# Inputs laid out with channels in the partitions, a token half of a residual added early, and layers' operands made in two steps

## The reference

```python
# first block
h = rms_norm(x, g_mix_pre);  proj = h @ w_in            # 2048 -> 9728
aq, ak, av, hq, hf, hi, hg, gate_a, gate_b = split(proj)
y_attn = sliding_window_attention(rotary(aq), rotary(ak), av, sinks)
y_hgrn = rms_norm(hgrn2_recurrence(hq, hf, hi, lb)) * silu(hg)
merged = sigmoid(gate_a) * (y_attn @ w_attn_branch) + sigmoid(gate_b) * (y_hgrn @ w_hgrn_branch)
x = x + rms_norm(merged @ w_out, g_mix_post)
gate, up = split(rms_norm(x, g_ffn_pre) @ w_gate_up)    # 2048 -> 2 * 5632
x = x + rms_norm((silu(gate) * up) @ w_down, g_ffn_post)
e = (p @ w_ple_proj) * sigmoid(rms_norm(x, g_ple_pre) @ w_ple_gate)
x = x + rms_norm(e, g_ple_post)
# second block, twice
shift, scale, gate = split(silu(c) @ w_ada[l] + b_ada[l])
h = layernorm(x) * (1 + scale) + shift;  u, z_f, cq, ckv, k_r, z_a = split(h @ w_in_2[l])
y = concat(fourier_mix(u) * silu(z_f), mla_attention(...) * silu(z_a)) @ w_out_2[l]
x = layernorm(alpha * x + gate * y, ln_g[l], ln_b[l])
```

## Time and profile before

| | us |
|---|---|
| median of 3 runs | 2225.4 (2224.73 to 2225.76) |
| profiled execution, whole | 2224.2 |
| its span | 2222.4 |
| TensorE busy | 2190.0 |
| VectorE busy | 1512.3 |
| ScalarE busy | 1104.5 |

### The profile page before, as it was taken

One profiled execution on the slowest core, in us unless ns is written; L12 is line 12 of the kernel. 1 busy time (PEld: TensorE's weight loads), 2 busy tenths in 40 slices (PEclk: granted clock), 3 DMA queues, 4 the chain that ended last, 5 costly groups with the idle time before them and its releaser, 6 DMA issues.

```text
span 2222.4 us, 26894 instructions
## 1 busy us (share of the span) xinstructions
PE 2190.0 (99%) x10449; PEld 1825.3 (82%) x10449; DVE 1512.3 (68%) x1963; ACT 1104.5 (50%) x1510; POOL 47.8 (2%) x68
## 2 busy tenths in 40 slices
PE   9999999999999999999999999999999999999997
PEld 7888888888888888888888888887898887788886
DVE  6675468768876777777777778766465566555556
ACT  6575456444445444444433444565465454546452
POOL 1000000100000000000000000000000000000000
PEclk9999999999999999999999999999999999999999
DMA  7544555499795889988889899573565572555563
GB/s 266 183 129 127 186 178 167 142 369 317 262 335 182 297 300 306 312 302 300 304 302 313 303 305 301 185 243 95 146 179 155 165 273 76 173 162 157 162 231 119
DMA packets 242607, 500.61 MB, mean 225 GB/s; under 512 B 17008, under 2 KB 26144, under 8 KB 241328
## 3 DMA queue, kind: packets, MB, share of 16 engines
q1 hardware_dynamic: 239088, 484.08, 65.7%
q0 software_dynamic: 3392, 14.82, 1.9%
HBM read 496.70 MB, written 2.12 MB: 224 GB/s over the span
## 4 chain that ended last, share of the span: by engine, by line
PE 92%; DVE 4%; ACT 2%; issue 1%; DMA 0%; POOL 0%; POOLq 0%; ACTq 0%; DVEq 0%
PE bank L898 89%; PE bank L901 3%; DVE wl L1875 1%; ACT arena L1324 1%; ACT wh L1324 1%; DVE arena L1878 1%; DVE arena L1883 0%; DVE arena L1882 0%; DMA raw<-in_w_ple_gate 0%; ACT hh L1324 0%; DVE al L1875 0%; DVE hl L1875 0%; POOL st L749 0%; DVE arena L1875 0%; ACT L1324 0%
## 5 line engine op out<-in xcount | busy, mean ns | idle before, releaser
L1324 ACT ACTIVATE wh<-raw 128x1024 fp32r<-128x1024 f32 (+2 forms) x500 | 520.2, 1043 | 660.7 <-PE bank L898 620.3
L1875 DVE TENSOR_TENSOR wl<-raw,wh 128x1024 fp32r<-128x1024 f32 (+2 forms) x500 | 599.9, 1202 | 336.5 <-ACT wh L1324 334.7
L898 PE MATMUL bank<-wh,hh 128*128 128x512 f32 (+1 forms) x1568 | 618.6, 396 | 7.3 <-DVE hl L1875 5.2
L898 PE MATMUL bank<-wl,hh 128*128 128x512 f32 (+1 forms) x1568 | 605.3, 387 | 0.0
L898 PE MATMUL bank<-wh,hl 128*128 128x512 f32 (+1 forms) x1568 | 605.2, 387 | 0.0
L898 PE MATMUL bank<-wh,ah 128*128 128x512 f32 (+1 forms) x1168 | 456.1, 391 | 2.5 <-ACT arena L1324 1.7
L898 PE MATMUL bank<-wh,al 128*128 128x512 f32 (+1 forms) x1168 | 450.9, 387 | 0.0
L898 PE MATMUL bank<-wl,ah 128*128 128x512 f32 (+1 forms) x1168 | 450.1, 386 | 0.0
L898 PEld LDWEIGHTS bank<-wh,hh 128*128 128x128 f32 x1568 | 295.4, 189 | 66.7 <-issue 10.0
L898 PEld LDWEIGHTS bank<-wh,hl 128*128 128x128 f32 x1568 | 294.3, 188 | 60.5
L898 PEld LDWEIGHTS bank<-wl,hh 128*128 128x128 f32 x1568 | 296.0, 189 | 55.5
(11 more groups left out here) (130 smaller groups left out, 1352.0 us busy)
## 6 DMA issues: line engine op xcount, KB each, us to landing
raw<-in_w_in SPq DMA_DIRECT2D x245, 512.0 KB, 3.7
arena<-in_w_ada SPq DMA_DIRECT2D x148, 384.0 KB, 5.0
arena<-in_w_gate_up SPq DMA_DIRECT2D x97, 512.0 KB, 4.6
raw<-in_w_ada SPq DMA_DIRECT2D x108, 384.0 KB, 4.8
raw<-in_w_out SPq DMA_DIRECT2D x80, 512.0 KB, 5.2
raw<-in_w_gate_up SPq DMA_DIRECT2D x79, 512.0 KB, 4.5
raw<-in_w_down SPq DMA_DIRECT2D x45, 512.0 KB, 5.2
arena<-in_w_down SPq DMA_DIRECT2D x43, 512.0 KB, 5.3
```

Source lines behind the costliest of these rows:

```text
L898: return i.matmul(o, l, x, start=start, stop=stop, skip_group_check=False)
L1324: return i.activation(o, x, fn, scale=scale, **k)
L1875: return i.tensor_tensor(o, a, b, op)
```

## The change

x comes in twice. A second input, `x_t`, is laid out by the host with the channel in the partition, 60 columns of gains ahead of it; it is loaded by pairs (256 KB, the first 286 KB with the columns) and goes straight into `x_split`, so `x_pair`, the transposes of g_mix_pre and TensorE's part of `tables` fall away. x in its natural layout is still loaded for the squares, in four parts behind items 6 to 9. Biases, c and the positions come in as columns too and are issued by POOL once x pair 3 has its high part. Unit 0 runs its three terms in the order high, weight low, operand low (was high, operand low, weight low). The keep at the start is now fourteen products of a tile of zeros, and ScalarE copies one column of it first. p is transposed by the host: `pn_t` only splits. In the last block of `wo` each token half gets its root as soon as it is done, and half 0 of the pieces 0 to 2 is added in the slots of half 1. In the layers `h_pair` of pairs 2 to 7 becomes `h_turn` (TensorE, ahead of slot p - 2), `h_affine` (behind the main work of slot p - 2) and `h_split` (ahead of slot p - 1); the norms 2 and 3 come one slot earlier.

```diff
 def timetable():
     ahead(-1, "begin")
-    ahead(0, "x_split", 1)
-    ahead(0, "x_split", 2)
-    for p in range(3, 8):
-        ahead(p - 2, "x_pair", p)
-        ahead(p - 2, "x_split", p)
-    start(3, "xstats")
-    start(5, "tables")
-    start(10, "q", 0)
-    start(10, "lb")
-    start(17, "q", 1)
+    ahead(0, "x_split", 0)
+    for p in range(1, 8):
+        ahead(p - 1, "x_split", p)
+    start(8, "xstats")
+    start(6, "tables")
+    start(13, "q", 0)
+    start(13, "lb")
...
     f = slot("gate", 0)
     ahead(f, "wo_end")
     ahead(f, "keep", 30, "ffn")
...
                 ahead(f, "ln_b", 0, 1, n)
         ahead(f, "pre", l)
-        for t, name, n in ((0, "norm", 0), (0, "norm", 1), (0, "h_pair", 0), (0, "h_pair", 1), (1, "h_pair", 2), (2, "norm", 2),
-                           (2, "h_pair", 3), (3, "h_pair", 4), (4, "norm", 3), (4, "h_pair", 5), (5, "h_pair", 6), (6, "h_pair", 7)):
+        for t, name, n in ((0, "norm", 0), (0, "norm", 1), (0, "h_pair", 0), (0, "h_pair", 1), (1, "norm", 2), (3, "norm", 3)):
             ahead(f + t, name, l, n)
+        for p in range(2, 8):
+            ahead(f + p - 2, "h_turn", l, p)
+            behind(f + p - 2, "h_affine", l, p)
+            ahead(f + p - 1, "h_split", l, p)
...
                     main(t)
+                for name, args in BEHIND.get(t, ()):
+                    if name in stages:
+                        stages[name](*args)
...
 
 
 
         def sp(e):
             i = e.i
-            i.dma_start(IDN, A["k_cst"][:, K_ID:K_ID + P]).then_inc(*S.d_id.dma())
...
+            def x_t(p):
+                a, b = 512 * p if p else -60, 512 * p + 512
+                i.dma_start(AR[:, 40 * 256 + a:40 * 256 + b], A["x_t"][:, 60 + a:60 + b]).then_inc(*S.get(f"d_xt{p}").dma())
+
+            def x_nat(c):
+                cs = slice(512 * c, 512 * c + 512)
+                i.dma_start(X0[:, :, cs], xd[:, :, cs]).then_inc(*S.get(f"d_x{c}").dma())
+
             item(0)
-            i.dma_start(X0[:, :, 512:1024], xd[:, :, 512:1024]).then_inc(*S.d_x1.dma())
-            item(1)
-            i.dma_start(X0[:, :, 1024:1536], xd[:, :, 1024:1536]).then_inc(*S.d_x2.dma())
-            item(2)
-            i.dma_start(X0[:, :, 1536:2048], xd[:, :, 1536:2048]).then_inc(*S.d_x3.dma())
-            item(3)
-            i.dma_start(CST[:, K_U:K_N], A["k_cst"][:, K_U:K_N]).then_inc(*S.d_cst.dma())
+            x_t(0)
+            for n in range(1, 4):
+                x_t(n)
+                item(n)
+            x_t(4)
+            item(4)
+            i.dma_start(CST[:, :], A["k_cst"]).then_inc(*S.d_cst.dma())
+            for n in range(5, 10):
+                if n < 8:
+                    x_t(n)
+                item(n)
+                if n > 5:
+                    x_nat(n - 6)
             i.dma_start(SINK, A["attn_sinks"].partition_broadcast(P).rearrange("p a n -> p (a n)")).then_inc(*S.d_sink.dma())
             i.dma_start(GN, A["hgrn_gnorm"].partition_broadcast(P).rearrange("p a n -> p (a n)")).then_inc(*S.d_gn.dma())
-            for n in range(4, len(ITEMS)):
...
+            e.wait_ge(*S.a_op.at("H1", 3))
+            i.dma_start(POSI, A["pos_col"]).then_inc(*S.d_pos.dma())
+            i.dma_start(CCOL[:, :], A["c_col"]).then_inc(*S.d_ccol.dma())
+            i.dma_start(BCOL[:, :], A["b_col"]).then_inc(*S.d_bcol.dma())
             i.dma_start(LB8, A["hgrn_lb_logits"].rearrange("a (p c) -> p a c", c=8)).then_inc(*S.d_lb8.dma())
...
+            def wo_root(m):
+                e.wait_ge(*S.v_rms.at("wo", m))
+                root(RSTD[:, m:m + 1], SSUM[:, m:m + 1], 1, S.g_rms.up("wo", m))
+
+            def wo_half():
+                wo_root(0)
+                yield
+
+            def wo_end():
+                wo_root(1)
...
-                e.wait_ge(*S.d_id.at())
-                keep(8, 0)
-                e.wait_ge(*S.d_stg.at())
-                tr(bank("gm", S.v_gm)[:, 0:16], STG, CST[0:16, K_ID:K_ID + 16]).then_inc(*S.p_gm.up())
-                e.wait_ge(*S.d_xa.at())
-                t_pair("H1", 0, X0[:, :, 0:256])
-                e.wait_ge(*S.d_xb.at())
-                t_pair("H1", 1, X0[:, :, 256:512])
-                keep(16, 1)
-
-            def x_pair(p):
-                e.wait_ge(*(S.d_x1, S.d_x2, S.d_x3)[p // 2 - 1].at())
-                t_pair("H1", p, X0[:, :, p * 256:(p + 1) * 256])
+                e.wait_ge(*S.v_zero.at())
+                bk = bank(("keep", 0), S.p_keep, 0)
+                for _ in range(14):
+                    x = mm(bk[:, 0:P], ZERO[:, 0:P], ZERO[:, 0:P], True, True)
+                x.then_inc(*S.p_keep.up(0))
 
...
-                if p < 2:
-                    t_pair(ph, p, nat)
-                    return
+                t_pair(ph, p, nat)
+
+            def h_turn(l, p):
+                e.wait_ge(*S.a_norm.at(l, p // 2))
+                e.wait_ge(*S.v_norm.at(l, p // 2))
+                ph, nat = f"H5{l}", TX[p // 2 % 2][:, :, p % 2 * 256:(p % 2 + 1) * 256]
                 for q, sig in enumerate((S.v_aff, S.a_aff)):
                     bk = bank((ph, p, q), sig, l, p)
...
             def begin():
-                e.wait_ge(*S.v_gm.at())
-                x_split(0)
+                e.wait_ge(*S.v_zero.at())
+                copy(ZERO[:, 129:130], ZERO[:, 128:129]).then_inc(*S.a_pre.up())
 
             def x_split(p):
-                split("H1", p, [GM[:, 2 * p:2 * p + 1], GM[:, 2 * p + 1:2 * p + 2]])
+                hi = pair_of("H1", p)[0]
+                e.wait_ge(*S.get(f"d_xt{p}").at())
+                copy(hi[:, 0, :], XT[:, 2 * p, :], scale=XCOL[:, 2 * p:2 * p + 1])
...
             def pn_t():
-                split("H4", 7)
+                e.wait_ge(*S.d_pn.at())
+                e.wait_ge(*S.p_unit.at(before("H4", 7)))
+                copy(pair_of("H4", 7)[0], PN).then_inc(*S.a_op.up("H4", 7))
...
+            def h_affine(l, p):
+                ph, T = f"H5{l}", TT2[p % 2].rearrange("p (k t) -> p k t", k=2)
+                scale, bias = h_columns(l, p)
+                e.wait_ge(*S.p_op.at(ph, p))
+                e.wait_ge(*S.v_op.at(ph, p - 2))
+                f(T[:, 1, :], BANK[bank_of[ph, p, 1]][:, 0:256], ACTF.Identity, scale=scale[1], bias=bias[1]).then_inc(*S.a_aff.up(l, p))
+
+            def h_split(l, p):
+                ph, T = f"H5{l}", TT2[p % 2].rearrange("p (k t) -> p k t", k=2)
+                e.wait_ge(*S.a_aff.at(l, p))
+                e.wait_ge(*S.v_aff.at(l, p))
+                h_free(ph, p)
+                copy(pair_of(ph, p)[0], T).then_inc(*S.a_op.up(ph, p))
 
             def u(l, n):
...
             def begin():
-                e.wait_ge(*S.p_gm.at())
-                then(i.tensor_copy(GM, BANK[bank_of["gm"]][:, 0:16]), S.v_gm)
-                x_split(0)
+                i.memset(ZERO, 0.0).then_inc(*S.v_zero.up())
 
             def x_split(p):
-                split("H1", p, [GM[:, 2 * p:2 * p + 1], GM[:, 2 * p + 1:2 * p + 2]])
+                hi, lo = pair_of("H1", p)
+                e.wait_ge(*S.a_op.at("H1", p))
+                stt(lo[:, 0, :], XT[:, 2 * p, :], XCOL[:, 2 * p:2 * p + 1], hi[:, 0, :].bitcast(F32), ALU.mult, ALU.subtract)
+                stt(lo[:, 1, :], XT[:, 2 * p + 1, :], XCOL[:, 2 * p + 1:2 * p + 2], hi[:, 1, :].bitcast(F32), ALU.mult,
+                    ALU.subtract).then_inc(*S.v_op.up("H1", p))
 
             def mean(n, *key):
 
...
-                e.wait_ge(*S.p_tab.at())
-                ps = BANK[bank_of["cols"]]
-                i.tensor_copy(COLS[:, 0:60], ps[:, 0:60])
-                i.tensor_copy(CCOL[:, :], ps[:, 384:512])
-                i.tensor_copy(BCOL[:, :], ps[:, 128:224])
-                then(i.tensor_copy(POS, ps[:, 256:260]), S.v_tab, "cols")
+                yield
+                e.wait_ge(*S.d_pos.at())
+                i.tensor_copy(COLS[:, 0:60], XCOL).then_inc(*S.v_col.up())
+                then(i.tensor_copy(POS, POSI), S.v_tab, "pos")
                 e.wait_ge(*S.d_cst.at())
                 yield
...
+            def wo_root(m):
+
+                o = SSUM[:, m:m + 1]
+                e.wait_ge(*S.a_sq.at("wo", 3, m))
+                then(red(o, SS[:, m:m + 1, :], ALU.add), S.v_rms, "wo", m, 0)
+                ts(o, o, 1.0 / D, EPS, ALU.mult, ALU.add).then_inc(*S.v_rms.up("wo", m))
+                then(wo_row(3, m), S.v_ev if m else S.v_evh, INDEX["wo", 3])
+
+            def wo_add(n, m):
+                cs = slice(n * 512, (n + 1) * 512)
+                e.wait_ge(*S.get(f"d_xr{n}").at())
+                e.wait_ge(*S.g_rms.at("wo", m))
+                return stt(XR[:, m, cs], YR[:, m, cs], RSTD[:, m:m + 1], XR[:, m, cs], ALU.mult, ALU.add)
+
             def wo_half():
-                wo_row(3, 0).then_inc(*S.v_evh.up(INDEX["wo", 3]))
-                yield
+                wo_root(0)
+                yield
+                wo_add(0, 0)
+                wo_add(1, 0)
+                yield
+                wo_add(2, 0)
 
             def wo_end():
```

(37 more changed lines are left out.)

134 lines of the change are left out of this document (55 added, 79 removed).

## The result

The kernel takes 2215.38 us (median of 4 runs, 2214.73 to 2215.86), where the kernel before takes 2225.58 (4 runs, 2224.73 to 2226.64): 0.9951 of it, interval 0.9939 to 0.9963. Forecast were 2215.6 us and a range of 2211.0 to 2220.3. The profiled execution took 2214.73 us around a span of 2212.9; the forecast for it was 2214.4.

The account below looks back on a forecast made before the run. TensorE, busy 2190 of 2222.4 us, was taken as the bound. Gains of 6.7 (start), 0.4 (output half), 0.4 (p) and 2.3 us (layers) sum to 9.8, bringing the median from 2225.4 to 2215.6 us, range 2211 to 2220.3.

Parts of the forecast that it names:

- The start: Kernel start through unit 17: earlier unit 1 2.6, removed TensorE work 4.7, less waits 0.6; 6.7 us gained, bounds 3 and 9.
- Unit 1: Second unit of the start: item 1 lands at 8.95 us, the unit begins at 11.2, 2.6 us earlier.
- The supply: Split weights at the start, with x loaded twice: on the edge at unit 10; all such waits 0.6 us, bounds 0 and 4.
- the weights stay 0.5 to 2 us ahead: Slots 9 to 14 of the start: engine work carried forward keeps split weights that far ahead of TensorE.
- The layers: First blocks of both layers: norms leave the serial cycle, 0.9 us each, plus 0.5 in layer 1; 2.3 us gained.
- The upper bound of 8.6 us: Both layers' first blocks: largest gain, if the new order frees the cycle altogether and units follow at TensorE's 3.19 us.
- The output half: Attention output to gate blocks: two adds become one, 0.67 us less, but keeps limit the gain to 0.4, bounds 0 and 0.6.
- A: Rival at the start: transfers bind, the second x eats the gain; start gives 3 us, total 2219.4; chance 0.18.
- B: Rival, more than forecast: item 1 lands at 7.3 us, layers give 3.5 each or clock is better; 2212.4 us; chance 0.15.
- C: Rival at the start: zeros fail to raise the clock by 7 us, unit 0 and part of 1 slow; 2217.1; chance 0.10.
- D: Rival, slower: late last x load delays the first eviction and unit 16's bank, about 5 us lost; 2230; chance 0.04.
- E: Rival, little effect: waits return, start gives 2 us, layers 0, halves 0.5; 2222.9 us; chance 0.05.

Follow-up runs that it names:

- l_old: The changed kernel with the layers' pairs 2 to 7 prepared in the old order again, norms 2 and 3 one slot later: 2218.68 us.
- l_early: The changed kernel with each layer affine moved ahead of its slot's main work, behind the split of the pair before: 2209.99 us.

## Why the prediction was right, and where it was off

**The time** came out 0.2 us from the forecast, and the terms outside the start within 0.25 us each, but for the 0.4 us ahead of the keeps that nothing had forecast. The start hides two misses of opposite sign, 0.7 us too little and 1.8 too much. That the whole came so close is in part luck: the start's miss of 1.1 us is mostly made up by this 0.4 and the small surpluses of the other terms.

**Unit 1** was forecast for 11.2 us, with item 1 landed at 8.95. It landed at 8.12 and unit 1 started at 10.51. The curve read from the landings before was somewhat slow; whether fewer, larger packets are the reason, no run shows. In the other profiles item 1 lands at 7.99 to 8.69 and unit 1 starts up to 11.08, so the value taken lies just beyond the slowest that was seen and the bound of 9.4 well beyond it. The first product's 7.1 was right by another cause: not the data (6.6) but the zeros set it, which end at 1.19 + 28 x 0.214 = 7.18 us. The prediction had named 7.0 as their worst case, and the worst case is what happened. It cost nothing, because unit 1 waited for item 1.

**The supply** is the term that was mis-sized: 0.6 us forecast, 2.4 measured (units 1 to 17 take 48.63, seventeen of 2.72 take 46.24). Its place was right: item 10 landed at 33.78 for a forecast of 33.5. What was off is the sum around it. Unit 1 came 0.7 us sooner, so unit 10 was wanted at 35.2 (it started at 36.28, 1.08 late) and not at 35.7; from the landing to the product it took 2.5 us and not 2.3. What was gained at unit 1 beyond the forecast was thus given back at unit 10, since item 10's landing and not unit 1 set it. The second part of the miss is the step "the weights stay 0.5 to 2 us ahead": units 13 and 16 were late too. Spreading the loads removed all three waits without a change to that work, so the two later ones followed from the first. The prediction had carried the later slots forward as if nothing were late at unit 10.

**The layers.** The cycle `wh`, `wl`, affine, `hh` was read rightly, and so were its size (3.39) and the share of the norm (0.45 twice a layer). Layer 0 gave 0.93 of 0.9. Undoing the order brought the 3.85 back, and so did putting only the affine behind the norm. One premise was not needed and mostly not so: "the high part of a weight waits for the unit before it". In layer 0 `wh` follows `hh` without idle time in every round from unit 3 on but one (it waits for TensorE at 1553.61, in the changed kernel at 1545.79); the cycle closes over ScalarE's own order. In layer 1, of the 1.63 for a forecast of 1.4, 0.53 lie in units 3 to 6, where a round of 3.85 went, and 1.10 in units 0 to 2, where one of 4.25 went. In the kernel with more keeps a round of 4.32 stands there again behind a faster unit 0, with nearly the same sum, so only the three units together count. The upper bound of 8.6 us, "if the order frees the cycle altogether", was not what this order does, but it is there to be had: with the early affine the two stretches take 46.03 us where the kernel before takes 54.58, or 8.55 less. The prediction had held that the affine behind `wl` keeps the cycle, and had not asked what it would be worth ahead of it.

**The output half.** 0.45 for 0.4, but for more reasons than given. The prediction put the gain down to the add that goes (0.67) and cut it to 0.4 because of the keeps. The runs show that the add alone is worth 0.16 with the keeps as they are, that the adds begin 0.29 sooner with a root for one half instead of two, and that another 0.4 lies behind the ten keeps.

**The rivals.** A (the second x eats the gain) had the right queue and the wrong reason: it cost 1.8 us more than forecast, not 3.7, and by its place, not by its bytes; with no second x at all the time is that with the loads spread. B's early landing came in part, and was given back. C did not occur, but narrowly: the profile's record of the granted clock begins at 7.17 us, at the upper level, and unit 0 at 7.18; in the other twelve the clock was up at 4.6 to 7.3 us. Its companion in B, that the layers' first units might gain 1.6 each at the upper level, is refuted for this kernel: with the upper level in both, nothing was gained from unit 0 on, and 0.46 us ahead of it in layer 1. D named the bank of unit 16 as the place, and TensorE did wait there, 0.5 us and not 5. E did not occur. The Trainium skill (DMA: Bandwidth & Descriptors, "Anatomy of one DMA") gives its 2.0 us and 436 GB/s for one transfer that GpSimd issues; the prediction applied them to several transfers queued by SP. So used they give 6.3 us for item 1; it landed at 8.12 here and at 8.48 with the loads spread out, so the rows of before were the better guide (8.95).

## What to carry to other kernels

A gain on one engine counts only up to the next thing that it waits for: the earlier unit 1 was given back at unit 10, the faster clock of unit 0 at units 1 and 2, the shorter adds to the keeps. So look, for each term, for what is due next, and carry its lateness forward. When a stage advances in even rounds longer than its TensorE work, write the round as a cycle over the engines and move an operation that needs nothing from the cycle out of it. Here moving the affine from behind one instruction of VectorE to ahead of it was worth more than half as much as the whole change. And look where in the queue a load stands that is not needed yet: here the same 2 MB cost 2.0 us behind items 6 to 9 and nothing behind items 7, 9, 11 and 12.

## What was not expected of the hardware

An fp32 product of 128 columns took 0.43 us in the zeros (28 records in 5.99 us for 14 products), close to the 2 x 0.227 that was thought an upper bound. All the time from 1.57 to 7.11 us the records stand 0.213 us apart. In ten of the other twelve profiles they stand 0.11 apart from some point on, and that is where the profile's record of the granted clock begins, at the upper level (4.72 us in l_old, 6.64 in l_early). So with the same zeros the clock came up anywhere between 4.7 and 7.3 us, and the first product began between 6.45 and 7.19.

With the same instructions in front of it, the stretch at the lower level of the clock ahead of a layer moved from kernel to kernel. In layer 0 with 58 keeps the granted clock fell between 0.1 and 2.8 us ahead of unit 0, or not at all (the two kernels with the early affines); in layer 1 with 82 keeps it fell 0.9 to 4.5 us ahead of it. What it costs depends on where it falls: on the transposes ahead of unit 0 it cost 0.46 us in layer 1 of the changed order, on unit 0 alone nothing that can be told. With 80 and 120 keeps it fell in none of the three profiles. How many keeps are needed was not tried, nor what moves the fall.
